# Turned activation blocks in natural token order, moved through a DRAM buffer instead of SBUF to SBUF

## The reference

```python
proj = rmsnorm(x, g_mix) @ w_in              # q, k, v of two attentions, an indexer, two gates
out_a = dsa_sparse_attention(...); out_b = forgetting_attention(...)
mixed = sigmoid(gate_a) * (out_a @ w_o_a) + sigmoid(gate_b) * (out_b @ w_o_b)
x = x + mixed @ w_out
h = rmsnorm(x, g_ffn)
x = x + (silu(h @ w_ffn_gate) * (h @ w_ffn_up)) @ w_ffn_down      # 5632 hidden channels
h = rmsnorm(x, g_ple)
x = x + sigmoid(h @ w_ple_gate) * (p @ w_ple_proj)
return rmsnorm(x, g_final)
```

## Time and profile before

| | |
|---|---|
| median of 3 runs | 1515.41 us (1515.39 to 1516.11) |
| the profiled execution | 1515.76 us, span 1513.9 us |
| matmuls | 6841, busy 1485.6 us (98%) |
| VectorE busy | 879.3 us (58%) |
| ScalarE busy | 691.0 us (46%) |
| granted TensorE clock | 0.998 of full speed |
| DMA | 290.91 MB, mean 192 GB/s |

### The profile page before, as it was taken

How to read it: one execution, slowest core, us unless ns; L and a number is a source line. 1 busy time by engine, 2 the same in 40 slices (tenths; PEclk the granted TensorE clock), 3 DMA queues, 4 the chain that set the end, 5 groups by cost and what they waited for, 6 DMA issues and landing times.

```text
span 1513.9 us, 19424 instructions
## 1 busy us (share of the span) xinstructions
PE 1485.6 (98%) x6841; PEld 1251.8 (83%) x6841; DVE 879.3 (58%) x1034; ACT 691.0 (46%) x846; POOL 49.9 (3%) x80
## 2 busy tenths in 40 slices
PE   5999999999999999999999999999999999999996
PEld 5888888889888888888888888888888888888885
DVE  6966776667655576655545554545555455454654
ACT  5544444544444544554444434444444343443544
POOL 0021001100210000000000000000000000000000
PEclk9999999999999999999999999999999999999999
DMA  6666565566555666766666666666666665666663
GB/s 190 187 193 175 175 191 181 164 187 187 168 167 175 193 207 221 226 208 182 214 202 202 201 200 188 197 205 204 198 204 194 196 197 184 206 198 192 216 204 107
DMA packets 182573, 290.91 MB, mean 192 GB/s; under 512 B 18744, under 2 KB 67824, under 8 KB 182000
## 3 DMA queue, kind: packets, MB, share of 16 engines
q1 hardware_dynamic: 172944, 281.02, 61.0%
q10 hardware_dynamic: 9568, 9.07, 2.0%
HBM read 275.87 MB, written 2.11 MB: 184 GB/s over the span
## 4 chain that ended last, share of the span: by engine, by line
PE 94%; DVE 3%; DMA 1%; ACT 1%; ACTq 1%; issue 0%; DVEq 0%
PE acc L1273 51%; PE acc L1278 25%; PE acc L1163 8%; PE acc L1172 4%; PE side L1273 2%; PE side L1278 1%; DVE ls L720 1%; ACTq L224 1%; DMA rope_c<-in_rope_rows 1%; PE side L1319 0%; DVE hn L775 0%; DMA ws<-in_w_out 0%; PE side L1325 0%; ACT hs L416 0%; PE side L1333 0%
## 5 line engine op out<-in xcount | busy, mean ns | idle before, releaser
L720 DVE TENSOR_TENSOR ls<-ws,hs 128x1024 fp32r<-128x1024 f32 (+1 forms) x520 | 628.6, 1223 | 550.3 <-ACT hs L416 546.7
L416 ACT ACTIVATE hs<-ws 128x1024 fp32r<-128x1024 f32 (+1 forms) x520 | 544.2, 1056 | 727.1 <-PE acc L1278 510.5
L1273 PE MATMUL acc<-hs,xg 128*128 128x512 f32 x1648 | 418.1, 395 | 0.0
L1273 PEld LDWEIGHTS acc<-hs,xg 128*128 128x128 f32 x1648 | 322.1, 195 | 62.6 <-DVE xg L1021 0.3
L1278 PE MATMUL acc<-ls,xg 128*128 128x512 f32 x824 | 225.7, 395 | 0.0
L1278 PEld LDWEIGHTS acc<-ls,xg 128*128 128x128 f32 x824 | 161.1, 195 | 31.2
L1273 PE MATMUL acc<-hs,ff 128*128 128x512 f32 x704 | 178.6, 396 | 0.0
L1273 PE MATMUL acc<-hs,hn 128*128 128x512 f32 (+1 forms) x704 | 171.9, 387 | 0.0
L1273 PEld LDWEIGHTS acc<-hs,ff 128*128 128x128 f32 x704 | 138.0, 196 | 26.3
L1273 PEld LDWEIGHTS acc<-hs,hn 128*128 128x128 f32 x704 | 127.1, 188 | 24.2
L1163 PE MATMUL acc<-hn,hs 128*128 128x512 f32 x560 | 139.3, 393 | 0.0
(11 more groups left out here) (192 smaller groups left out, 811.8 us busy)
## 6 DMA issues: line engine op xcount, KB each, us to landing
ws<-in_w_in SPq DMA_DIRECT2D x152, 512.0 KB, 3.9
ws<-in_w_ffn_gate SPq DMA_DIRECT2D x88, 512.0 KB, 4.4
ws<-in_w_ffn_up SPq DMA_DIRECT2D x88, 512.0 KB, 4.4
ws<-in_w_ffn_down SPq DMA_DIRECT2D x88, 512.0 KB, 3.9
ws<-in_w_out SPq DMA_DIRECT2D x32, 512.0 KB, 4.7
ws<-in_w_ple_gate SPq DMA_DIRECT2D x32, 512.0 KB, 4.2
ws<-in_w_o_b SPq DMA_DIRECT2D x16, 512.0 KB, 4.4
ws<-in_w_o_a SPq DMA_DIRECT2D x16, 512.0 KB, 4.6
```

What stands on the lines that cost most here:

```text
L416: act.activation(hs[:, j, 0:n], ws[:, j, 0:n], ACT.Copy).then_inc(h_split, 1)
L720: dve.tensor_tensor(ls[:, j, 0:n], ws[:, j, 0:n], hs[:, j, 0:n].bitcast(F32), ALU.subtract).then_inc(l_split, 1)
L1273: pe.matmul(banks[b], block_of(src, k, part, b), hs[:, slot, q * width:(q + 1) * width], start=first and q == 0 and part == 0, stop=False)
```

## The change

The turned tiles get natural token order: `mixed`, `xg`, `ff` are laid out as [part, tile, 256 tokens], so that a block of 128 tokens is 128 elements in a row. The moves from SBUF to SBUF are gone, and with them all of SP's. ScalarE instead writes `t_rows` whole (128 partitions x 4 KB) into a DRAM buffer `quads` after splitting chunks 4 and 5 (`park_quads`), and after splitting chunks 6 and 7 waits for that write (`parked`) and reads it back with four DMAs, each for 32 partitions of `t_cols` with 4 pieces of 1 KB a partition (`fetch_quads`). `MOVES` goes from 16 to 4. The low parts of `xg` are made with two instructions of 128 elements for each tile instead of one of 256.

```diff
-MOVES = QUADS * QUADS
+MOVES = QUADS
...
-    xg = sb("xg", 16, [KT, 2 * TOK], F32R)
+    xg = sb("xg", 16, [2, KT, TOK], F32R)
...
-    mixed = sb("mixed", 48, [KT, 2 * TOK], F32R)
-    ff = sb("ff", 48, [KT_FF, 2 * TOK], F32R)
+    mixed = sb("mixed", 48, [2, KT, TOK], F32R)
+    ff = sb("ff", 48, [2, KT_FF, TOK], F32R)
...
-    t_cols = sb("t_cols", 184, [QUADS, 4, QUAD, 2])
+    t_cols = sb("t_cols", 184, [QUADS, 4, 2, QUAD])
-    t_rows = sb("t_rows", 196, [QUADS, 4, QUAD, 2])
+    t_rows = sb("t_rows", 196, [QUADS, 4, 2, QUAD])
...
-        return t[:, :, :, :, :].rearrange("p a k n b -> p k a (n b)")
+        return t[:, :, :, :, :].rearrange("p a k b n -> p (k b) a n")
...
-        return t.rearrange("p k (a n) -> p k a n", a=QUADS)
-
-    def move_quads(eng, t, odd):
-
-        eng.wait_ge(turned, 2 * t + 2)
-        for a in range(QUADS):
-            for q in range(odd, QUADS, 2):
-                eng.dma_start(t_cols[QUAD * q:QUAD * (q + 1), a, :, :, :],
-                              t_rows[QUAD * a:QUAD * (a + 1), q, :, :, :]).then_inc(moved, 16)
+        return t.rearrange("p k (b a n) -> p (k b) a n", b=2, a=QUADS)
+
+    t_apart = quads.rearrange("(a i) (q m) -> q i a m", a=QUADS, q=QUADS)
...
-            if i > 0:
-                move_quads(sp, T_MIX + i - 1, 0)
...
-            move_quads(sp, T_MIX + N_WIDE - 1 + i, 0)
...
-                if half == 0:
-                    move_quads(sp, T_FF - 1 + i, 0)
...
-                if c == K_CH - 1:
-                    move_quads(sp, T_PLE - 1 + n, 0)
...
-                if n == 0 and c == K_CH - 1:
-                    move_quads(sp, T_PLE + N_WIDE - 1, 0)
...
+        def park_quads(t):
+
+            act.wait_ge(turned, 2 * t + 2)
+            act.dma_start(quads, t_rows[:, :, :, :, :].rearrange("p q k b n -> p (q k b n)")).then_inc(parked, 16)
+
+        def fetch_quads(t):
+
+            act.wait_ge(parked, 16 * (t + 1))
+            for q in range(QUADS):
+                act.dma_start(t_cols[QUAD * q:QUAD * (q + 1), :, :, :, :].rearrange("p a k b n -> p a (k b n)"),
+                              t_apart[q]).then_inc(moved, 16)
+
         def split_and_move(first, t):
 
             split_chunks(first, 2)
-            move_quads(act, t, 1)
+            park_quads(t)
             split_chunks(first + 2, 2)
+            fetch_quads(t)
...
-                dve.transpose(t_rows[:, :, :, :, b].rearrange("p q k n -> p k q n"),
+                dve.transpose(t_rows[:, :, :, b, :].rearrange("p q k n -> p k q n"),
...
-                dve.scalar_tensor_tensor(in_quads(xg[:, k:k + 1, TOK:2 * TOK]), by_tile(t_cols)[:, m:m + 1],
-                                         gains[:, KT * (stage + 1) + k:KT * (stage + 1) + k + 1],
-                                         in_quads(xg[:, k:k + 1, 0:TOK].bitcast(F32)), ALU.mult, ALU.subtract).then_inc(xg_ready, 1)
+                gain = gains[:, KT * (stage + 1) + k:KT * (stage + 1) + k + 1]
+                for b in range(2):
+                    ins = dve.scalar_tensor_tensor(in_quads(xg[:, 1, k:k + 1, :])[:, b], by_tile(t_cols)[:, 2 * m + b], gain,
+                                                   in_quads(xg[:, 0, k:k + 1, :].bitcast(F32))[:, b], ALU.mult, ALU.subtract)
+                ins.then_inc(xg_ready, 1)
...
-            return src[:, k, part * TOK:(part + 1) * TOK].rearrange("p (n b) -> p b n", b=2)[:, b, :]
+            return src[:, part, k, b * P:(b + 1) * P]
```

More of the change, by code:

```diff
@@ L110, in leave, with hybrid_layer @@
         self.fixed, self.moving = self.start + end * self.steps, 0
-def hybrid_layer(nc, c_rows, x, p, positions, g_mix, w_in, b_f, w_o_a, w_o_b, w_out, g_ffn, w_ffn_gate,
+def hybrid_layer(nc, c_rows, quads, x, p, positions, g_mix, w_in, b_f, w_o_a, w_o_b, w_out, g_ffn, w_ffn_gate,
                  w_ffn_up, w_ffn_down, g_ple, w_ple_gate, w_ple_proj, g_final, rope_rows, out):
@@ L255, in hybrid_layer @@
     p_t, p_high, p_ready = S("p_t"), S("p_high"), S("p_ready")
-    turned, moved = S("turned"), S("moved")
+    turned, parked, moved = S("turned"), S("parked"), S("moved")
     ff_silu, ff_s, ff_high, ff_ready = map(S, ("ff_silu", "ff_s", "ff_high", "ff_ready"))
@@ L560, in split_chunks @@
                 split_high(at // SLOTS, at % SLOTS)
+        def park_quads(t):
[6 more added lines that the diff above has]
+                              t_apart[q]).then_inc(moved, 16)
         def split_and_move(first, t):
             split_chunks(first, 2)
-            move_quads(act, t, 1)
+            park_quads(t)
             split_chunks(first + 2, 2)
+            fetch_quads(t)
         def mixed_high(n):
             act.wait_ge(moved, 16 * MOVES * (T_MIX + n + 1))
-            act.activation(in_quads(mixed[:, 4 * n:4 * n + 4, 0:TOK]), by_tile(t_cols), ACT.Copy).then_inc(mix_high, 1)
+            act.activation(in_quads(mixed[:, 0, 4 * n:4 * n + 4, :]), by_tile(t_cols), ACT.Copy).then_inc(mix_high, 1)
         act.wait_ge(gate_out, 2 * N_WIDE)
@@ L597, in new_high @@
                 k = 4 * n + m
-                act.activation(in_quads(xg[:, k:k + 1, 0:TOK]), by_tile(t_cols)[:, m:m + 1], ACT.Copy,
+                act.activation(in_quads(xg[:, 0, k:k + 1, :]), by_tile(t_cols)[:, 2 * m:2 * m + 2], ACT.Copy,
                                scale=gains[:, KT * (stage + 1) + k:KT * (stage + 1) + k + 1]).then_inc(xg_high, 1)
@@ L621, in ff_pair @@
             split_high(u + 1, 1)
-            move_quads(act, T_FF - 1 + c, 1)
+            park_quads(T_FF - 1 + c)
             split_high(u + 1, 2)
             split_high(u + 1, 3)
+            fetch_quads(T_FF - 1 + c)
             if first:
@@ L645, in ff_hi @@
             act.wait_ge(moved, (c + T_FF + 1) * (16 * MOVES))
-            act.activation(in_quads(ff[:, ds(c * 4, 4), 0:TOK]), by_tile(t_cols), ACT.Copy).then_inc(ff_high, 1)
+            act.activation(in_quads(ff[:, 0, ds(c * 4, 4), :]), by_tile(t_cols), ACT.Copy).then_inc(ff_high, 1)
         ff_pair(0, 0, first=True)
@@ L993, in mixed_low @@
             dve.wait_ge(mix_high, n + 1)
-            dve.tensor_tensor(in_quads(mixed[:, 4 * n:4 * n + 4, TOK:2 * TOK]), by_tile(t_cols),
-                              in_quads(mixed[:, 4 * n:4 * n + 4, 0:TOK].bitcast(F32)), ALU.subtract).then_inc(mix_ready, 1)
+            dve.tensor_tensor(in_quads(mixed[:, 1, 4 * n:4 * n + 4, :]), by_tile(t_cols),
+                              in_quads(mixed[:, 0, 4 * n:4 * n + 4, :].bitcast(F32)), ALU.subtract).then_inc(mix_ready, 1)
         for n in range(N_WIDE):
@@ L1087, in ff_low @@
             dve.wait_ge(ff_high, c + 1)
-            dve.tensor_tensor(in_quads(ff[:, ds(c * 4, 4), TOK:2 * TOK]), by_tile(t_cols),
-                              in_quads(ff[:, ds(c * 4, 4), 0:TOK].bitcast(F32)), ALU.subtract).then_inc(ff_ready, 1)
+            dve.tensor_tensor(in_quads(ff[:, 1, ds(c * 4, 4), :]), by_tile(t_cols),
+                              in_quads(ff[:, 0, ds(c * 4, 4), :].bitcast(F32)), ALU.subtract).then_inc(ff_ready, 1)
         ff_pair(0, 0, first=True)
@@ L1486 @@
     c_rows = nc.dram_tensor("c_rows", (HB, TOK), F32, kind="Internal").ap()
-    hybrid_layer(nc, c_rows, *args, out)
+    quads = nc.dram_tensor("quads", (P, 2 * WIDE), F32, kind="Internal").ap()
+    hybrid_layer(nc, c_rows, quads, *args, out)
     r = run_bass_kernel_spmd(nc, [arrays], core_ids=[0])
```

## The result

The changed kernel takes 1535.37 us (four runs, 1530.95 to 1539.38) against 1515.53 for the kernel before: ratio 1.013, 95% interval 1.010 to 1.016, **slower by 19.8 us**, where 22.8 us less were forecast. The profiled execution is the slowest of the four, 1539.38, span 1537.6; its span is 23.7 us longer than that of before.

A forecast was written before the change was run, and what follows sets the result against it. TensorE's matmul count and start spacing were taken as the bound. -26.2 for the step, +1.8 for `mixed`, +1.5 and +0.1 for `xg` gave -22.8 us: 1492.6 us from 1515.41, range 1488 to 1502.

The forecast's parts named there:

- Point 1: TensorE's chunks of `mixed`, `xg` and `ff`: without the step of two, 2.72 us each for 2.80, 328 chunks, -26.2 us.
- second rival: The step of two costs nothing, so only the additions of 3.4 us are left: 1518.8 us, slower; chance 0.06.
- Point 2: SP's queue: 8 DMA issues a strip fewer, some 5.0 us, in 23 strips; 0 on the path, loads less bunched.
- Point 4: Trip through DRAM and two added waits: write 4.1 us, last read 2.5; no cost from chunk 8's split in most strips.
- upper bound, 8.8: Highest landing time in us allowed for the last read of a strip, taken from the slowest weight load.
- rival of 0.13: ScalarE starves TensorE at chunk 8 of all 23 strips; at 8.8 write and 4.3 read, 1573 us; chance 0.13.
- Point 5: Where the turned strip is wanted at once: last `mixed` strip +1.8 us; last `xg` strip before the FFN also stalls.
- slack of 0.7: Spare us before chunk 8's split would delay TensorE, in the three strips inside the `w_o` stage; cost still 0.
- 3.0 elsewhere: Spare us between chunk 8's split and TensorE wanting it, outside the `w_o` stage; no cost in most strips.
- Point 6: `xg` low parts on VectorE as two instructions each: two tiles 1.4 us at most for 1.0; 0 cost elsewhere.
- third rival: In-order waits on ScalarE before chunk 8's split starve TensorE in all 23 strips, 23 us per further us; chance 0.13.
- slower side: Starving of TensorE in every strip that leaves the kernel slower or at zero gain; chance 0.05.

## Why the prediction was wrong

**Point 1, the step, was right.** 2.72 us a chunk and 188 to 189 ns a load; alone it gives 25.4 us where 26.2 were summed. The second rival falls. So does, for TensorE's weight load of this kernel, the Trainium skill's rule (Advanced Engine Details and Errata, SBUF Cachelines): two hits to a 16-byte line did not give the full rate here; the trace disagrees by 6.7 ns a matmul.

**Point 2 failed, and it is the cause.** It priced SP's freed queue at 0 and called the loads "less bunched beside the small transfers". I looked at what the removed issues cost SP, and not at what they held back. While SP stood in its moves for 5 us a strip, no weight load left. Freed, it sends 512 KB for every chunk into the very stretch in which the strip is on its way. Three runs show it from three sides: SP held until the strip has landed, 1501.6; SP held until the write has landed and the reads on its own queue, 1489.0; the old moves with SP free, 7 us worse and landings of 4.3 for 1.9.

**Point 4's term for the read was mis-sized by that:** for the 2.5 taken, the last read of a strip landed in 6.9 us at the median (5.2 over all four) and 9.9 at most; with SP held it took 2.8, so the 2.5 was near for an empty stretch. I took the price "near the move, for its size"; the move's 1.9 had been measured in the quiet that the change took away. The upper bound, 8.8, was reached in the strip of the 8.0 us stall and passed in another, but the range of the forecast left it out, and the rival of 0.13 took 4.3 for the read. The write (3.4 for 4.1) and its cover by two splits were right, and the issue of the reads was priced too high (0.45 each for 0.61).

**Point 5** followed: stalls of 8.0 and 6.5 for the 2.3 and 1.8 forecast. The slack of 0.7 in the three `w_o` strips was overrun by about 3 us each, the 3.0 elsewhere in seven strips by 0.5 to 2.6. **Point 6** was right in size: the four low parts of a strip took 2.19 us for 1.68, and the wait of the weight loads for `xg` went from 0.3 to 1.4 with the order alone.

**The third rival** had place and mechanism right (in-order waits in front of chunk 8), for half of the waits. With landings of 3.4 and 6.9 its formula gives 0.7 us in each of 23 strips, 16 in all; measured were 18.1, but in ten strips, and 17.4 more where the turned strip itself was wanted. Its slower side had a chance of 0.05. **Not in any sum** was the clock: the chunks behind the stalls ran at 1.2 GHz in part, some 14 us in all.

## What to carry to other kernels

An issue that is taken off a queue takes away its delay of what stands behind it too: ask what that queue will send in its place, and beside which transfer. A landing time read from a trace holds for the traffic of its moment, so price a new transfer in the traffic that the change leaves. Try a small transfer that is wanted soon on the queue of the bulk loads, ahead of them, with none of them under way when it leaves: that was the best place here, and beside them on another queue the worst.

## What the runs showed of the hardware that I had not expected

- Four reads of 32 partitions on ScalarE's queue landed in 5.2 us (median) beside weight loads issued by SP, and in 2.8 on SP's own queue with none under way ahead of them and 3 or 4 weight loads of 512 KB directly behind.
- Beside weight loads, how many partitions a read reaches counted for more than the size of its pieces: four reads of 128 partitions x 1 KB made a kernel of 1524.9 us, four of 32 x 4 KB one of 1538.5.
- A TensorE wait of 8 us took the granted clock from 1.00 to 0.50 (2.4 to 1.2 GHz), and the chunk after it was 2.0 us longer.
